# A transformer kernel on one core: the next phase's first transposes move from in front of the last six products to behind them

## The chip, the cores and the metric

The kernel runs on one NeuronCore of a Trainium2 chip. The metric is the device time of one execution in microseconds (us). The engines that matter are TensorE (PE in the profile; its weight loads are shown apart, as PEld), VectorE (DVE), ScalarE (ACT), GpSimd (POOL) and the queue of SyncE (SP), which issues most of the weight transfers.

## The reference

256 tokens of width 1024 pass through two blocks of two layers each. Cut to what matters:

```python
# first block, per layer
h = h + mixer(rms_norm(h, mix_norm_g[layer]))           # layer 0: gated chunk mixer, layer 1: dilated attention
h = h + square(relu(rms_norm(h, mlp_norm_g[layer]) @ w_up[layer])) @ w_down[layer]
...
# second block, per layer: three sub-layers, each modulated and gated by a condition
h = modulate(rms_norm(x, norm_g[i, s]), shift[:, s], scale[:, s])
x = x + gate[:, s] * sub_layer(h)                       # swiglu, then pool or conv mixer, then swiglu
```

All of it is float32. Every sub-layer begins with a norm over the 1024 values of a token, and ends with a product whose output is added to the residual stream.

## The kernel before, in words

The kernel is written engine by engine; each engine runs its own list of instructions in order, and semaphores tie them together. The 256 tokens are two tiles of 128 (t = 0 and t = 1). Weights come from HBM as slabs of 1 MB into a ring of five slots; a slot's next load is issued by the SP queue when PE has raised `slab_used`. ScalarE makes a rounded copy of a slab (`w_hi`, L498) and VectorE the remainder (`w_lo`, L831), and every product is three matmuls of 128x512 (hi by hi, hi by lo, lo by hi).

The work is a row of phases: `gate_in`, `gate_out`, `mlp0`, `qkv`, `attn`, `attn_out`, `mlp1`, `ffn0`, `pool`, `ffn1`, `ffn2`, `conv_in`, `conv_out`, `ffn3`. At the end of a phase PE finishes the accumulators `acc`: tile 0, first half of the columns, then its second half, then tile 1 in the same two halves. A half of one slab is six matmuls (two rows of weights, three matmuls each). That is `down_halves` (L1329), called from `down_last` (L1348) and at the end of `ffn` (L1652).

What follows a finished half:

- VectorE adds it to the residual stream `res` (L943; in the second block it first multiplies by the gate, L940). Each half raises `acc_ready`, the last one of all `slab_used`.
- ScalarE squares tile 0 (L518), GpSimd makes the reciprocal root (L470, L464), VectorE scales the tile into `xn` (L847) and raises `xn_ready`.
- PE transposes `xn` of tile 0 in eight transposes (`turn_norm(name, 0)`, L1388, recorded as L1376), four to a bank of `tr_ps`.
- ScalarE scales the transposed pieces back into `xn` (`norm_out`, L531 in the first block, L533 in the second), and VectorE splits them into `xT_hi` (L860) and `xT_lo` (L861), two of eight pieces at a time (`norm_split`).
- The first up product of the next phase (`first_chunk`, L1396) waits for the first two pieces (`xT_ready`), then multiplies 18 times, and then come the eight transposes of tile 1.

VectorE's list at such a border is written out in `enter` (L863). In its usual form it is:

```python
scale_tokens(NORM[name], 0)
products(1, 0)
norm_split(name, 0, (0, 2))
products(1, 1)
norm_split(name, 0, (4, 6))
scale_tokens(NORM[name], 1)
norm_split(name, 1)
```

Where `between` was given to `down_halves`, PE runs `turn_norm(next, 0)` between the two halves of tile 1: six matmuls, eight transposes, six matmuls, then the first up product. That is so at six borders: into `mlp0`, `qkv`, `mlp1`, `ffn2`, `conv_in` and `ffn3`. At two borders, into `ffn0` (where `early` is False) and into `ffn1`, the transposes already follow the last product.

Of the kernel before, what the change touches and what calls it, by code (L numbers as in the profile page):

```python
# [159 lines left out]
def build(nc, x, mix_norm_g, mlp_norm_g, final_norm_g, a_w_in, a_ln_g, a_ln_b, a_w_s, a_b_s, a_w_out,  # L160
# [7 lines left out]
    with ctx:  # L168
# [16 lines left out]
        xT_hi = sb("xT_hi", [P, KT, TOKENS], F32R)  # L185
        o_tok = nc.alloc_sbuf_tensor_at("o_tok", [P, TT, HEADS * HD], F32, offset=xT_at)
        xT_lo = sb("xT_lo", [P, KT, TOKENS], F32R)
# [3 lines left out]
        hT_hi = sb("hT_hi", [P, 4, TOKENS], F32R)  # L191
        hT_lo = sb("hT_lo", [P, 4, TOKENS], F32R)
# [62 lines left out]
        hi_ready, lo_ready, slab_used = sem("hi_ready"), sem("lo_ready"), sem("slab_used")  # L255
# [33 lines left out]
        XT = {n: i for i, n in enumerate(n for n in XN if n not in ("pool", "final2"))}  # L289
# [992 lines left out]
        def _(pe):  # L1282
# [43 lines left out]
                                      stop=stop and q == DOWNK - 1 and x_part is lo)  # L1326
                return last

            def down_halves(g, t, hi, lo, k0, between=None):  # L1329

                for c in range(2):
                    if c and between is not None:
                        between()
                    last = down_tile(g, t, hi, lo, k0, False, (c,), True)
                    if (t, c) != (TT - 1, 1):
                        last.then_inc(acc_ready, 1)
                return last
# [7 lines left out]
                    last = down_tile(g, t, hi, lo, k0, start)  # L1345
                last.then_inc(slab_used, 1)

            def down_last(g, hi, lo, k0, start, ready=None, between=None):  # L1348


                for t in range(TT):
                    if ready is not None:
                        pe.wait_ge(tr_read, ready[0] + (t + 1) * ready[1])
                    if t == 0:
                        pe.wait_ge(lo_ready, g + 1)
                    last = down_tile(g, t, hi, lo, k0, start)
                    if t == 1:
                        last.then_inc(slab_used, 1)
                    else:
                        pe.wait_ge(lo_ready, g + 2)  # L1360
                    last = down_halves(g + 1, t, hi, lo, k0 + 2, between if t else None)
                last.then_inc(slab_used, 1)

            def bank(tr):

# [22 lines left out]
            def turn_norm(name, t):  # L1388

                for b in range(KT // FILL):  # L1390
                    pe.wait_ge(xn_ready, 4 * XN[name] + 2 * t + b + 1)
                    if (t, b) == (0, 0):
                        pe.wait_ge(tr_read, at[name].tr)
                    turn(xn, t, b * FILL, FILL, at[name].tr + (KT // FILL) * t + b)
# [24 lines left out]
            g = at["gate_in"].slab  # L1419
            first_chunk("gate_in", turned=False)  # L1420
            for c in range(1, 4):
                up_chunk(g + 2 * c, free=(gelu_done, 2 * (c - 1) + 1))
                if c == 1:
                    p = at["positions"]
# [7 lines left out]
                    for n in range(NG):  # L1432
                        c0 = n * VLEN
                        while c0 < (n + 1) * VLEN:
                            c1 = min((n + 1) * VLEN, (c0 // 512 + 1) * 512)
                            last = mm(acc[0:HEADS, c0 // D, c0 % D:c0 % D + c1 - c0], rel[:, n * HEADS:(n + 1) * HEADS],
                                      mask_sb[:, n, c0 - n * VLEN:c1 - n * VLEN], start=True, stop=True)
# [4 lines left out]
            for t in range(TT):  # L1442
                pe.wait_ge(vn_ready, t + 1)
                for q in range(GROUPS):
                    last = mm(acc[:, t, q * P:(q + 1) * P], ws_T[:, q, :], g_v[:, t, q * P:(q + 1) * P],
                              start=True, stop=True)
                last.then_inc(mix_ready, 1)
            p = at["gate_out"]
            for n in range(NORM_FILLS):
                t, b = divmod(n, KT // FILL)  # L1450
                pe.wait_ge(gated, t + 1)
                turn(xn, t, b * FILL, FILL, p.tr + n)
            for k in range(2):
                down_slab(p.slab + k, xT_hi, xT_lo, 2 * k, k == 0, (p.tr, 2))
            down_last(p.slab + 2, xT_hi, xT_lo, 4, False, (p.tr, 2), lambda: turn_norm("mlp0", 0))

            def modulation(name, sub, half):

# [6 lines left out]
                        last = nc.tensor.transpose(dst[:, f * P:(f + 1) * P], ada_acc[:, n * P:(n + 1) * P], ident)  # L1465
                    last.then_inc(tr_ready, 1)

            def mlp(name, after, early=True):
                p = at[name]
                m0 = 0 if name == "mlp0" else MLP_CHUNKS  # L1470
                g = p.slab

                def turn_mid(c, t):
                    pe.wait_ge(mlp_mid, 2 * (m0 + c) + t + 1)
                    turn(mid, t, 0, 4, mid_fill(p, name, c) + t)

                def between(s, t):
                    if (s, t) == (0, 0):
                        for t in range(TT):
                            turn_mid(0, t)  # L1480
                    elif s == 1:
                        for sub in MODS.get(name, ()):
                            modulation(name, sub, t)

                first_chunk(name)
                for c in range(1, MLP_CHUNKS - 1):
                    gb = g + 4 * c - 2
                    up_chunk(gb, (relu_done, 2 * (m0 + c - 1) + 1), between if c == 1 else None)
                    for s in range(2):
                        down_slab(gb + 2 + s, hT_hi, hT_lo, 2 * s, c == 1 and s == 0,  # L1490
                                  (mid_fill(p, name, c - 1), 1))
                    for t in range(TT):
                        turn_mid(c, t)

                c = MLP_CHUNKS - 1
                gb = g + 4 * c - 2
                up_chunk(gb, (relu_done, 2 * (m0 + c - 1) + 1))
                down_slab(gb + 2, hT_hi, hT_lo, 0, False, (mid_fill(p, name, c - 1), 1))
                pe.wait_ge(lo_ready, gb + 4)
                down_tile(gb + 3, 0, hT_hi, hT_lo, 2, False)  # L1500
                turn_mid(c, 0)
                down_tile(gb + 3, 1, hT_hi, hT_lo, 2, False).then_inc(slab_used, 1)
                turn_mid(c, 1)
                down_last(gb + 4, hT_hi, hT_lo, 0, False, (mid_fill(p, name, c), 1),
                          (lambda: turn_norm(after, 0)) if early else None)
                if not early:
                    turn_norm(after, 0)

            mlp("mlp0", "qkv")

            p = at["qkv"]
# [10 lines left out]
            for i in range(2):  # L1522
                for b in range(3):
                    c = 3 * i + b
# [61 lines left out]
            pe.wait_ge(o_ready, 2 * HEADS)  # L1586
            for t in range(TT):
                turn(o_tok, t, 0, 4, p.tr + t, order=flip[:, 0, :])
            down_last(p.slab, hT_hi, hT_lo, 0, True, (p.tr, 1), lambda: turn_norm("mlp1", 0))

            mlp("mlp1", "ffn0", False)

            def gate(sub):

# [8 lines left out]
            def ffn(name, after):  # L1603
                p = at[name]
                f0 = FFN_AT[name] * FFN_CHUNKS
                g = p.slab
                mods = MODS.get(name, ())

                def turn_mid(c, t):
                    pe.wait_ge(ffn_mid, 2 * (f0 + c) + t + 1)  # L1610
                    turn(mid, t, 0, 2, mid_fill(p, name, c) + t)

                def between(s, t):
                    if (s, t) == (0, 0):
                        for m in GATES[name]:
                            gate(m)
                        for t in range(TT):
                            turn_mid(0, t)
                    elif t != s:
                        for m in mods[:1]:  # L1620
                            modulation(name, m, s)

                first_chunk(name)
                for c in range(1, FFN_CHUNKS - 1):
                    gb = g + 3 * c - 1
                    up_chunk(gb, (ffn_mid, 2 * (f0 + c - 1) + 1), between if c == 1 else None)
                    if c == 1:

                        pe.wait_ge(gate_ready, GATES[name][-1] + 1)
                        for m in mods[1:]:  # L1630
                            modulation(name, m, 0)
                    down_slab(gb + 2, hT_hi, hT_lo, 0, c == 1, (mid_fill(p, name, c - 1), 1))
                    if c == 1:
                        for m in mods[1:]:
                            modulation(name, m, 1)
                    for t in range(TT):
                        turn_mid(c, t)

                c = FFN_CHUNKS - 1
                gb = g + 3 * c - 1  # L1640
                up_chunk(gb, (ffn_mid, 2 * (f0 + c - 1) + 1))
                ready = mid_fill(p, name, c - 1)
                turn_mid(c, 0)
                pe.wait_ge(lo_ready, gb + 3)
                down_tile(gb + 2, 0, hT_hi, hT_lo, 0, False)
                turn_mid(c, 1)
                pe.wait_ge(lo_ready, gb + 4)
                pe.wait_ge(tr_read, ready + 3)
                down_halves(gb + 3, 0, hT_hi, hT_lo, 2)
                down_tile(gb + 2, 1, hT_hi, hT_lo, 0, False).then_inc(slab_used, 1)  # L1650
                pe.wait_ge(tr_read, ready + 4)
                down_halves(gb + 3, 1, hT_hi, hT_lo, 2,  # L1652
                            (lambda: turn_norm(after, 0)) if after in XT else None).then_inc(slab_used, 1)

            ffn("ffn0", "pool")
            p = at["pool"]
# [55 lines left out]
                pe.wait_ge(conv_lo, k + 1)  # L1712
                down_slab(g + k, xT_hi, xT_lo, 2 * k, k == 0)
            pe.wait_ge(conv_lo, 4)
            down_last(g + 2, xT_hi, xT_lo, 4, False, between=lambda: turn_norm("ffn3", 0))
            ffn("ffn3", "final2")


# [23 lines left out]
```

## Time and profile before

| | |
|---|---|
| median of 3 runs | 1597.26 us (1595.93 to 1598.85) |
| the profiled execution: its time | 1596.6 us |
| the profiled execution: its span | 1594.8 us |
| PE busy | 1523.5 us, 96% of the span |
| VectorE, ScalarE, GpSimd busy | 66%, 45%, 2% |
| mean granted TensorE clock | 0.984 of full |

The span is the time from the first to the last instruction of the profiled execution; 1.8 us lie around it. A busy PE is not a PE at its peak: a matmul is counted from its start to its end, and the next begins before that end.

### The profile page before, as it was taken

How to read it: one execution, taken by the hardware profiler on the slowest of the kernel's cores; microseconds unless marked ns; L12 is line 12 of the kernel's file. 1: busy time of each engine (PE TensorE's matmuls, PEld its weight loads, DVE VectorE, ACT ScalarE, POOL GpSimd, SP SyncE). 2: the span in 40 equal slices, each digit the busy share in tenths (PEclk: the TensorE clock that was granted, in tenths of full speed). 3: DMA queues.
4: the chain of work that ended last, by engine and by line, in shares of the span. 5: the costliest groups of instructions: out<-in, count | busy, mean ns of one | idle time of the engine just before them, and what ended most of it. 6: DMA issues, size and time to landing. Idle time of an engine off the chain costs nothing.

```text
span 1594.8 us, 17438 instructions
## 1 busy us (share of the span) xinstructions
PE 1523.5 (96%) x7069; PEld 1249.8 (78%) x7069; DVE 1047.8 (66%) x1220; ACT 713.4 (45%) x879; POOL 32.9 (2%) x63
## 2 busy tenths in 40 slices
PE   5999999999899999899999799999999999999998
PEld 4778888888787888678888678887788878778886
DVE  5658766645448677577888668788644465774444
ACT  6345444533444454444343434445344454454442
POOL 1000000000000000000000000000000000000000
PEclk9999999999899999999999899999999999999999
DMA  7449777557326877748988168987455555355552
GB/s 258 160 147 327 272 265 281 173 171 251 125 69 243 290 290 271 249 138 303 322 297 282 52 228 309 324 296 264 140 185 185 187 174 193 134 183 185 185 186 91
DMA packets 202203, 346.19 MB, mean 217 GB/s; under 512 B 9563, under 2 KB 105059, under 8 KB 202124
## 3 DMA queue, kind: packets, MB, share of 16 engines
q1 hardware_dynamic: 161708, 267.22, 48.7%
q10 hardware_dynamic: 40416, 77.86, 13.5%
q8 instruction: 56, 0.92, 0.2%
q14 instruction: 23, 0.19, 0.0%
HBM read 343.96 MB, written 1.09 MB: 216 GB/s over the span
## 4 chain that ended last, share of the span: by engine, by line
PE 80%; DVE 9%; DMA 4%; ACT 3%; issue 1%; POOL 1%; SPq 0%; DVEq 0%; POOLq 0%; ACTq 0%
PE up_ps L1284 48%; PE acc L1284 27%; PE tr_ps L1376 3%; DVE w_lo L831 3%; DMA raw<-in_ffn_w_in 2%; ACT w_hi L498 2%; PE tr_ps L1284 1%; DVE ada_acc L904 1%; DMA raw<-in_w_down 1%; DVE res L943 1%; DVE xn L940 1%; DMA raw<-in_w_up 1%; PE tr_ps L1558 1%; ACT xn L518 1%; DVE xT_lo L861 1%
## 5 line engine op out<-in xcount | busy, mean ns | idle before, releaser
L831 DVE TENSOR_TENSOR w_lo<-raw,w_hi 128x2048 fp32r<-128x2048 f32 x245 | 559.3, 2289 | 289.9 <-ACT w_hi L498 289.7
L498 ACT ACTIVATE w_hi<-raw 128x2048 fp32r<-128x2048 f32 x245 | 469.1, 1918 | 287.8 <-DMA raw<-in_ffn_w_in 132.3
L1284 PE MATMUL up_ps<-w_hi,xT_hi 128*128 128x512 f32 x1264 | 504.1, 399 | 13.4 <-DVE xT_lo L861 7.4
L1284 PE MATMUL up_ps<-w_hi,xT_lo 128*128 128x512 f32 x1264 | 495.5, 392 | 0.0
L1284 PE MATMUL up_ps<-w_lo,xT_hi 128*128 128x512 f32 x1264 | 494.9, 392 | 0.0
L1284 PEld LDWEIGHTS up_ps<-w_hi,xT_hi 128*128 128x128 f32 x1264 | 239.2, 189 | 67.6 <-issue 9.5
L1284 PEld LDWEIGHTS up_ps<-w_hi,xT_lo 128*128 128x128 f32 x1264 | 238.8, 189 | 51.4
L1284 PEld LDWEIGHTS up_ps<-w_lo,xT_hi 128*128 128x128 f32 x1264 | 239.5, 189 | 47.0
L1284 PE MATMUL acc<-w_hi,hT_hi 128*128 128x512 f32 x624 | 199.9, 394 | 5.7 <-DVE hT_lo L841 5.7
L1284 PE MATMUL acc<-w_hi,hT_lo 128*128 128x512 f32 x624 | 197.9, 391 | 0.0
L1284 PE MATMUL acc<-w_lo,hT_hi 128*128 128x512 f32 x624 | 197.7, 391 | 0.0
L904 DVE SCALAR_TENSOR_TENSOR ada_acc<-ada_raw,cond,ada_acc 128x512 f32<-128x512 f32 x252 | 189.1, 751 | 12.8 <-DMA ada_raw<-in_ada_w 5.1
L1284 PEld LDWEIGHTS acc<-w_hi,hT_hi 128*128 128x128 f32 x624 | 117.1, 189 | 30.2 <-DVE hT_lo L841 5.6
L508 ACT ACTIVATE hT_hi<-tr_ps 128x256 fp32r<-128x256 f32 (+1 forms) x122 | 48.3, 441 | 199.1 <-PE tr_ps L1376 195.5
L1284 PEld LDWEIGHTS acc<-w_hi,hT_lo 128*128 128x128 f32 x624 | 117.7, 189 | 24.8
L1284 PEld LDWEIGHTS acc<-w_lo,hT_hi 128*128 128x128 f32 x624 | 117.8, 189 | 24.5
L732 ACT ACTIVATE pre<-up_ps 128x256 f32<-128x256 f32 x88 | 33.4, 382 | 142.8 <-PE up_ps L1284 142.6
L841 DVE TENSOR_TENSOR hT_lo<-tr_ps,hT_hi 128x256 fp32r<-128x256 f32 (+1 forms) x122 | 55.7, 492 | 46.0 <-ACT hT_hi L508 45.5
L1138 DVE TENSOR_TENSOR mid<-pre,up_ps 128x256 f32<-128x256 f32 x88 | 35.0, 415 | 49.6 <-ACT pre L732 49.6
L518 ACT ACTIVATE xn<-res 128x512 f32<-128x512 f32 x48 | 30.6, 638 | 56.7 <-DVE res L943 48.6
L1376 PEld LDWEIGHTS tr_ps<-flip,mid 128*128 128x128 f32 x304 | 36.8, 140 | 14.1 <-issue 4.2
L1376 PE MATMUL tr_ps<-flip,mid 128*128 128x128 f32 x304 | 44.5, 273 | 2.7 <-DVE mid L1138 1.4
(123 smaller groups left out, 810.4 us busy)
## 6 DMA issues: line engine op xcount, KB each, us to landing
raw<-in_ffn_w_in SPq DMA_DIRECT2D x176, 512.0 KB, 4.8
ada_raw<-in_ada_w ACTq DMA_DIRECT2D x72, 1024.0 KB, 7.1
raw<-in_ffn_w_out SPq DMA_DIRECT2D x88, 512.0 KB, 4.4
raw<-in_w_up SPq DMA_DIRECT2D x64, 512.0 KB, 5.4
raw<-in_w_down SPq DMA_DIRECT2D x64, 512.0 KB, 4.3
raw<-in_b_w_qkv SPq DMA_DIRECT2D x36, 512.0 KB, 4.4
raw<-in_conv_w_in SPq DMA_DIRECT2D x24, 512.0 KB, 4.5
raw<-in_a_w_in SPq DMA_DIRECT2D x16, 512.0 KB, 7.5
```

The source lines that it names most:

```text
L498: nc.scalar.activation(w_hi[:, slot, :], raw[:, slot, :], ACT.Copy).then_inc(hi_ready, 1)
L508: nc.scalar.activation(dst, src, ACT.Copy).then_inc(tr_hi, 1)
L518: nc.scalar.activation(xn[:, t, cols], res[:, t, cols], ACT.Square, scale=D ** -0.5, accum_out=sumsq[:, t, c:c + 1]).then_inc(sumsq_ready[ ...
L732: nc.scalar.activation(pre[:, t, 0:HALF], up_ps[:, t, 0:HALF], ACT.Silu).then_inc(silu_done, 1)
L831: nc.vector.tensor_tensor(w_lo[:, slot, :], raw[:, slot, :], w_hi[:, slot, :].bitcast(F32), ALU.subtract).then_inc(lo_ready, 1)
L841: nc.vector.tensor_tensor(lo, src, hi.bitcast(F32), ALU.subtract).then_inc(tr_read, 1)
L861: nc.vector.tensor_tensor(lo, src, hi.bitcast(F32), ALU.subtract).then_inc(xT_ready, 1)
L904: a = nc.vector.scalar_tensor_tensor(out=dst, in0=src, scalar=cond[:, k:k + 1], in1=dst, op0=ALU.mult, op1=ALU.add)
L940: own(nc.vector.scalar_tensor_tensor(out=xn[:, t, cols], in0=src, scalar=gate, in1=gate_B[:, sub % 3, cols], op0=ALU.mult, op1=ALU.mult))
L1138: nc.vector.tensor_tensor(mid[:, t, 0:HALF], pre[:, t, 0:HALF], up_ps[:, t, HALF:UPN], ALU.mult).then_inc(ffn_mid, 1)
L1284: return nc.tensor.matmul(dst, a, b, start=start, stop=stop, skip_group_check=True)
L1376: last = nc.tensor.transpose(dst[:, q * P:(q + 1) * P], tile, ident)
```

## The change

`down_halves` loses its argument `between`, so that all twelve matmuls of tile 1's two halves stand one behind the other. `turn_norm(next, 0)` is called after them: in `down_last` through the new argument `after`, at the end of `ffn` directly. The argument `early` of `mlp` goes, because both orders are now the same. The six borders named above change; the ones into `ffn0`, `pool` and `ffn1` stay as they were. No instruction is added or taken away, and no other engine's list changes.

```diff
-            def down_halves(g, t, hi, lo, k0, between=None):
+            def down_halves(g, t, hi, lo, k0):
                 for c in range(2):
-                    if c and between is not None:
-                        between()
                     last = down_tile(g, t, hi, lo, k0, False, (c,), True)
                     if (t, c) != (TT - 1, 1):
                         last.then_inc(acc_ready, 1)
...
-            def down_last(g, hi, lo, k0, start, ready=None, between=None):
+            def down_last(g, hi, lo, k0, start, ready=None, after=None):
...
-                    last = down_halves(g + 1, t, hi, lo, k0 + 2, between if t else None)
+                    last = down_halves(g + 1, t, hi, lo, k0 + 2)
                 last.then_inc(slab_used, 1)
+                if after is not None:
+                    turn_norm(after, 0)
...
-            down_last(p.slab + 2, xT_hi, xT_lo, 4, False, (p.tr, 2), lambda: turn_norm("mlp0", 0))
+            down_last(p.slab + 2, xT_hi, xT_lo, 4, False, (p.tr, 2), "mlp0")
...
-                          (lambda: turn_norm(after, 0)) if early else None)
-                if not early:
-                    turn_norm(after, 0)
+                          after)
...
-                down_halves(gb + 3, 1, hT_hi, hT_lo, 2,
-                            (lambda: turn_norm(after, 0)) if after in XT else None).then_inc(slab_used, 1)
+                down_halves(gb + 3, 1, hT_hi, hT_lo, 2).then_inc(slab_used, 1)
+                if after in XT:
+                    turn_norm(after, 0)
```

The calls for `mlp1` and `ffn3` change in the same way as the one for `mlp0`.

## Rows read from the trace of the kernel before

**Rows 1.** Page, the chain that ended last: shares of the span by engine

```profile
PE 80%; DVE 9%; DMA 4%; ACT 3%; issue 1%; POOL 1%; SPq 0%; DVEq 0%; POOLq 0%; ACTq 0%
```

**Rows 2.** Chain in order of time, border into `mlp0`: start us, us, what

```profile
106.64 0.87 PE tr_ps L1376 x8
107.52 1.39 PE acc L1284 x6
```

**Rows 3.** Timeline, border into `mlp0`: start us, us, engine, line, what, count, idle before

```profile
106.03 0.39 PE L1284 MATMUL acc<-w_lo,xT_hi 128*128 128x512 f32 x1
...
106.25 0.39 PE L1284 MATMUL acc<-w_hi,xT_lo 128*128 128x512 f32 x1
...
106.48 1.03 PE L1376 MATMUL tr_ps<-flip,xn 128*128 128x128 f32 x8
...
107.27 0.47 PE L1284 MATMUL acc<-w_hi,xT_hi 128*128 128x512 f32 x1
...
107.78 0.29 DVE L860 CAST xT_hi<-xn 128x256 fp32r<-128x256 f32 x1 [0.41 <-ACT xn L531]
...
108.64 0.19 PEld L1284 LDWEIGHTS up_ps<-w_hi,xT_hi 128*128 128x128 f32 x1 [0.17 <-issue]
108.74 0.41 PE L1284 MATMUL up_ps<-w_hi,xT_hi 128*128 128x512 f32 x1
```

**Rows 4.** Timeline, border into `ffn3`, PE and VectorE

```profile
1394.85 0.39 PE L1284 MATMUL acc<-w_hi,xT_lo 128*128 128x512 f32 x1
...
1395.12 1.09 PE L1376 MATMUL tr_ps<-flip,xn 128*128 128x128 f32 x8
...
1396.09 0.69 DVE L943 TENSOR_TENSOR res<-res,xn 128x512 f32<-128x512 f32 x1
...
1397.62 0.47 PE L1284 MATMUL up_ps<-w_hi,xT_hi 128*128 128x512 f32 x1
```

**Rows 5.** Timeline, border into `conv_in`, PE and VectorE

```profile
1295.59 0.39 PE L1284 MATMUL acc<-w_hi,hT_lo 128*128 128x512 f32 x1
...
1296.96 1.09 PE L1376 MATMUL tr_ps<-flip,xn 128*128 128x128 f32 x8 [0.98 <-DVE xn L847]
...
1297.93 0.69 DVE L943 TENSOR_TENSOR res<-res,xn 128x512 f32<-128x512 f32 x1
```

**Rows 6.** Timeline, border into `ffn2`, PE

```profile
1095.90 0.39 PE L1284 MATMUL acc<-w_hi,hT_lo 128*128 128x512 f32 x1
...
1097.30 1.09 PE L1376 MATMUL tr_ps<-flip,xn 128*128 128x128 f32 x8 [1.01 <-DVE xn L847]
```

**Rows 7.** Timeline, border into `ffn0`, where the transposes already stand last, PE

```profile
671.41 1.09 PE L1376 MATMUL tr_ps<-flip,xn 128*128 128x128 f32 x8 [1.18 <-DVE xn L847]
...
673.90 0.47 PE L1284 MATMUL up_ps<-w_hi,xT_hi 128*128 128x512 f32 x1 [1.40 <-DVE xT_lo L861]
```

**Rows 8.** Chain in order of time, start of `mlp1`

```profile
484.16 0.33 SPq L331
...
484.53 7.24 DMA raw<-in_w_down
```

**Rows 9.** Timeline, start of `mlp1`, ScalarE's queue and PE's two waits

```profile
480.05 0.38 ACTq L567 DMA_DIRECT2D ada_raw<-in_ada_w  x1
...
496.79 1.16 PE L1465 MATMUL tr_ps<-flip,ada_acc 128*128 128x128 f32 x8 [0.89 <-DVE hT_lo L841]
...
503.21 1.60 PE L1465 MATMUL tr_ps<-flip,ada_acc 128*128 128x128 f32 x8 [2.49 <-DVE mod_sum L915]
```

**Rows 10.** Timeline, second chunk of `ffn3`, PE

```profile
1411.38 0.47 PE L1284 MATMUL up_ps<-w_hi,xT_hi 128*128 128x512 f32 x1 [1.18 <-DVE mid L1138]
```

**Rows 11.** Windows: stretch, us, busy of PE, PEld, DVE, ACT, POOL, granted clock, DMA share, GB/s

```profile
672.00:676.00 4.00, 2.60 (x11) 2.02 (x10) 1.38 (x4) 3.84 (x11) 0.00 (x0) 0.80 0.94 349
676.00:680.00 4.00, 2.83 (x9) 1.91 (x9) 2.51 (x6) 1.66 (x6) 1.17 (x3) 0.77 0.77 309
...
1296.00:1300.00 4.00, 3.04 (x17) 2.37 (x18) 3.48 (x9) 2.29 (x7) 0.38 (x1) 1.00 0.69 256
```

More of the change, by code:

```diff
@@ L1466, in modulation, with mlp @@
                     last.then_inc(tr_ready, 1)
-            def mlp(name, after, early=True):
+            def mlp(name, after):
                 p = at[name]
@@ L1588, in _ @@
                 turn(o_tok, t, 0, 4, p.tr + t, order=flip[:, 0, :])
-            down_last(p.slab, hT_hi, hT_lo, 0, True, (p.tr, 1), lambda: turn_norm("mlp1", 0))
-            mlp("mlp1", "ffn0", False)
+            down_last(p.slab, hT_hi, hT_lo, 0, True, (p.tr, 1), "mlp1")
+            mlp("mlp1", "ffn0")
             def gate(sub):
@@ L1714, in _ @@
             pe.wait_ge(conv_lo, 4)
-            down_last(g + 2, xT_hi, xT_lo, 4, False, between=lambda: turn_norm("ffn3", 0))
+            down_last(g + 2, xT_hi, xT_lo, 4, False, after="ffn3")
             ffn("ffn3", "final2")
```

## The prediction

> **What bounds the kernel now.** I read the page first, for the chain that ended last: 80% of the span lies on PE [rows 1]. So a microsecond in which PE has nothing to issue is a microsecond of the kernel, unless a later wait of PE takes it up. Then I asked for the chain in order of time at each of the eight borders between phases, and for the timeline of every engine there. In the first block (`mlp0`, `qkv`, `mlp1`) the chain runs through PE alone: eight transposes, six matmuls, the next phase [rows 2]. At the six matmuls' side ScalarE and VectorE turn the transposes' results into the first pieces of `xT`, and these are ready just as the six end: the weight load of the first up product waits 0.17 us, the product itself starts at the usual pitch [rows 3]. At the borders into `ffn2` and `conv_in` it is otherwise: PE waits 1.01 and 0.98 us for VectorE's `xn` before the transposes can begin [rows 5, 6]. Last I read PE's waits in the 40 us behind each border, for anything that could take up a delay.
>
> **The unit of the sum.** Matmuls of 128x512 in a stream start 0.225 us apart (106.03 to 106.25, and 106.48 for what follows) [rows 3]. Six of them are 6 x 0.225 = 1.35 us. From the first transpose to the first up product it is 108.74 - 106.48 = 2.26 us in `mlp0` [rows 3], and 1397.62 - 1395.12 = 2.50 us in `ffn3` [rows 4]. The second is the longer because there a scale and a shift are applied. I call this stretch the chain: transposes, ScalarE, VectorE. Before, six matmuls lay inside it. After, they lie in front of it, and nothing lies inside but the transposes.
>
> **What is removed, added and moved.** No instruction goes or comes. Six times, eight transposes move behind six matmuls on PE's list. No DMA is issued by them, and no list of another engine changes. The first up product of the next phase then starts at: start of the transposes now, plus how much later they start, plus the chain.
>
> - `mlp0`, `qkv`, `mlp1`. `xn` is ready when PE comes to the transposes (no wait stands at 106.48, and VectorE has gone on to `res`) [rows 3]; the pattern is the same three times. After, the transposes start 1.35 us later and the chain is as long as now: +1.35 us each, 4.05 us. The chain's bare length is not shown here, since the matmuls end with it. From below: the weight load at 108.64 is 0.10 us ahead of the product, of which 0.03 would remain, so at least 2.19 us [rows 3] and +1.28 us each. From above: `ffn0`, where nothing covers the chain already, has 673.90 - 671.41 = 2.49 us [rows 7], with the extra shift in it: +1.58 us each. I take 1.35, because the row of the same border is nearer than that of another kind of phase, and because the first matmul after a wait lasts 0.47 us where it lasts 0.41 in a stream [rows 3, 4], which gives back what the lower bound saves.
> - `ffn3`. The six would run from 1394.85 + 0.225 to 1396.43; the transposes start 1.31 us later than at 1395.12 [rows 4]. Eight transposes straight behind matmuls take 1.03 us [rows 3], behind a wait 1.09 [rows 4], so the chain is about 0.06 shorter: +1.25 us.
> - `ffn2` and `conv_in`. Here the six matmuls fill a wait that PE has anyway. In `conv_in` they end at 1295.59 + 0.225 + 1.35 = 1297.17 against a start of the transposes at 1296.96: +0.21 us [rows 5]. In `ffn2` they end at 1095.90 + 1.58 = 1097.48 against 1097.30: +0.18 us [rows 6]. Against that stands that VectorE is busy with the product of the half before until 1297.93 + 0.69 = 1298.62 [rows 5], so part of it is hidden, and the transposes start faster behind matmuls. Bounds 0 and 0.2; I take 0.1 each, 0.2 together. What PE won in front of the transposes it gives back behind them.
>
> Sum: 4.05 + 1.25 + 0.2 = 5.5 us. With all low bounds 3 x 1.28 + 1.25 = 5.1 us, with all high ones 3 x 1.58 + 1.31 + 0.39 = 6.4 us.
>
> **What comes after a border.** The transposes of tile 1 stand 18 up matmuls behind the first up product, and VectorE's list puts the last half's residual behind the first split of tile 0. All of it moves by the same amount, and I find nothing that catches up. The last half is finished earlier by the transposes' share: it ends at 108.91 now [rows 2], and would at 106.48 + 5 x 0.225 + 0.39 = 108.00. So the last slot of the ring comes free 0.9 us earlier, and its load starts earlier while PE starts later. No PE wait in this trace is shown to hang on that load (see the second rival).
>
> **Rivals.**
>
> - The waits at the start of `mlp1` take up that border's delay. PE waits 0.89 and 2.49 us there [rows 9]. If what it waits for did not move, 1.35 us would vanish and the sum be 4.1 us: 1601.4 us. Against it: the chain leads from the second wait back to a transfer that SP issues at 484.16, when a slab of the new phase is released, and which takes 7.24 us behind the 2 MB that ScalarE's queue asked for from 480.05 on [rows 8, 9]. Both issues follow the border and move with it. Chance 0.1.
> - The other side, not slower: weights decide behind the border. If the earlier release of 0.9 us counted at the waits of `mlp1` and at the 1.18 us wait in `ffn3` [rows 9, 10], PE would leave them 0.9 us earlier than now instead of 1.35 and 1.25 later, and the sum would be 1.35 + 1.35 - 0.9 - 0.9 + 0.2 = 1.1 us: 1598.4 us, no measurable difference. It decides once more than 2.3 of the 5.5 us are taken up. Against it: the same issue time as above, and in `ffn3` PE waits for `mid` of VectorE, whose list leads back to the border. Chance 0.06.
> - The bare waits cost clock. At `ffn0`, where PE waits 1.18 us, transposes for 1.09 and waits 1.40 [rows 7], the granted clock reads 0.80 and 0.77 over the next 8 us: part of it at 1.2 GHz instead of 2.4, a loss of 4 x 0.20 + 4 x 0.23 = 1.7 us of work [rows 11]. At the changed borders PE would transpose for about 1.03 and wait for about 1.2 to 1.4 us. One border would add 1.7 (1604.5 us), the four that now wait bare 6.8 (1609.6 us). Against it: `conv_in` has the mirror image now, a wait of 0.98 and then the transposes, at a full clock [rows 5, 11]. Chance 0.1. [...]
>
> **How the numbers follow.** The profiled execution took 1596.6 us (span 1594.8, 1.8 around it), 0.7 below the median of 1597.26. Against its own time the change gives 1602.1 us; against the median 1597.3 + 5.5 = 1602.8 us, which I forecast, with a chance of 0.72 and a range of its own from 1601.0 to 1605.0 (the bounds 5.1 and 6.4, and the spread of the three runs, about 1.5 us either way). The remaining 0.02 is for causes I don't see. A measurement of this kernel can tell about 0.2%, or 3.2 us, from no change; 5.5 us is 0.34%. The first rival is still slower, the second within 0.2%, the third slower. Some of the forecast's and of the first rival's cases fall under 3.2 us by the spread of runs. That makes 0.85 slower, 0.12 within, 0.03 faster. For the range, I go down past the first rival to 1599.3 and up to one or two borders with a lower clock, 1607.0.
>
> **What the profile would show.** At 106 us PE should issue twelve matmuls without a break, then eight transposes, and then have an idle stretch of about 1.2 us ended by `xT_lo` of VectorE, four times (`mlp0`, `qkv`, `mlp1`, `ffn3`). At `ffn2` and `conv_in` the wait for `xn` of about 1 us should be gone and one of some 1.3 us stand behind the transposes. The busy time of PE should hardly change. The start of the phases should move by 1.35, 2.7, 4.05, 4.15, 4.25 and 5.5 us. Wrong would prove me: waits behind a border that shrink by what the border lost, a first up product that starts less than 2.1 us behind the first transpose, or a granted clock below 1 right behind a changed border.

## The result, and the profile after

The kernel after takes 1605.78 us in the median of 10 runs (1600.53 to 1608.47), the kernel before 1598.01 us in 10 runs beside it (1594.7 to 1602.66). The ratio is 1.0040, with a 95% interval of 1.0023 to 1.0058: slower by 0.4%. Timed a second time (`e5_after_again` below) it was 1.0030 (1.0017 to 1.0042). The forecast was 1602.8 us with a range of 1599.3 to 1607.0, or 0.34% slower.

The page of the profiled execution of after, which took 1606.02 us:

```profile
span 1604.3 us, 17438 instructions
...
PE 1524.5 (95%) x7069; PEld 1251.6 (78%) x7069; DVE 1048.5 (65%) x1220; ACT 715.7 (45%) x879; POOL 32.9 (2%) x63
...
PE 81%; DVE 8%; DMA 5%; ACT 3%; issue 1%; POOL 0%; SPq 0%; DVEq 0%; POOLq 0%; ACTq 0%
```

The same number of instructions, the same busy time on PE, a longer span: the added time is time in which PE waits. The chain in order of time shows it at the border into `mlp0`, where it had run through PE alone [rows 2]:

```profile
99.80 7.71 PE acc L1284 x34
107.51 0.45 PE tr_ps L1376 x4
...
107.98 0.64 ACT xn L531 x2
...
108.64 0.30 DVE xT_hi L860
...
108.97 0.44 DVE xT_lo L861
...
109.54 2.51 PE up_ps L1284 x10
```

Now the chain leaves PE after the first bank of four transposes, goes through two ScalarE instructions and two of VectorE, and comes back. PE's timeline there, which answers to [rows 3]:

```profile
107.12 0.39 PE L1284 MATMUL acc<-w_hi,xT_lo 128*128 128x512 f32 x1
107.35 1.03 PE L1376 MATMUL tr_ps<-flip,xn 128*128 128x128 f32 x8
109.51 0.19 PEld L1284 LDWEIGHTS up_ps<-w_hi,xT_hi 128*128 128x128 f32 x1 [1.37 <-issue]
109.54 0.47 PE L1284 MATMUL up_ps<-w_hi,xT_hi 128*128 128x512 f32 x1 [1.16 <-DVE xT_lo L861]
...
109.85 0.39 PE L1284 MATMUL up_ps<-w_lo,xT_hi 128*128 128x512 f32 x1
```

And at the borders into `conv_in` and `ffn3`, which answer to [rows 5] and [rows 4]:

```profile
1303.85 0.40 PE L1284 MATMUL acc<-w_hi,hT_lo 128*128 128x512 f32 x1
1304.08 1.04 PE L1376 MATMUL tr_ps<-flip,xn 128*128 128x128 f32 x8
1306.52 0.47 PE L1284 MATMUL up_ps<-w_hi,xT_hi 128*128 128x512 f32 x1 [1.40 <-DVE xT_lo L861]
...
1404.35 0.40 PE L1284 MATMUL acc<-w_hi,xT_lo 128*128 128x512 f32 x1
1404.58 1.04 PE L1376 MATMUL tr_ps<-flip,xn 128*128 128x128 f32 x8
1407.02 0.47 PE L1284 MATMUL up_ps<-w_hi,xT_hi 128*128 128x512 f32 x1 [1.40 <-DVE xT_lo L861]
```

In `conv_in` the wait of 0.98 us in front of the transposes [rows 5] is gone, and one of 1.40 us stands behind them. Below, a wait in which PE has nothing at all to issue is called bare.

**A ruler for one border.** Single executions of either kernel spread over 8 us, so one span says little about 1.35 us. GpSimd's timeline is a better ruler: at each border it makes the root of tile 0 before the changed place and the root of tile 1 behind it, and the distance of the two is that border's length, whatever happened earlier. At `mlp0`, first before, then after:

```profile
104.53 0.56 POOL L464 TENSOR_TENSOR rstd<-msq,neg_half 128x1 f32<-128x1 f32 x1
...
111.28 0.56 POOL L464 TENSOR_TENSOR rstd<-msq,neg_half 128x1 f32<-128x1 f32 x1
```

```profile
104.03 0.56 POOL L464 TENSOR_TENSOR rstd<-msq,neg_half 128x1 f32<-128x1 f32 x1
...
112.15 0.56 POOL L464 TENSOR_TENSOR rstd<-msq,neg_half 128x1 f32<-128x1 f32 x1
```

6.75 us became 8.12: + 1.37 us. The same reading at all six borders, for after and for every experiment (us added against before):

| kernel | mlp0 | qkv | mlp1 | ffn2 | conv_in | ffn3 | sum |
|---|---|---|---|---|---|---|---|
| after | 1.37 | 1.36 | 1.36 | 0.16 | 0.16 | 1.35 | 5.76 |
| e5_after_again | 1.38 | 1.37 | 1.36 | 0.15 | 0.15 | 1.35 | 5.76 |
| e1_first_block | 1.38 | 1.36 | 1.37 | 0.01 | 0.01 | 0.01 | 4.14 |
| e2_ffn2_conv_in | 0.01 | 0.00 | 0.00 | 0.14 | 0.17 | 0.01 | 0.33 |
| e3_three_behind | 0.69 | 0.69 | 0.68 | 0.01 | 0.01 | 0.67 | 2.75 |
| e4_filled | 1.37 | 1.36 | 1.36 | 0.16 | 0.16 | 1.35 | 5.76 |
| e6_filled_again | 1.37 | 1.36 | 1.37 | 0.18 | 0.16 | 1.35 | 5.79 |
| e7_twelve_behind | 1.02 | 1.00 | 1.02 | 3.31 | 2.24 | 2.23 | 10.82 |
| e8_before_kept_busy | 0.01 | 0.01 | 0.01 | 0.01 | 0.01 | 0.01 | 0.06 |
| e9_after_kept_busy | 1.37 | 1.37 | 1.37 | 0.15 | 0.14 | 1.35 | 5.75 |

Where one of these six borders was left unchanged, it repeats to 0.01 us. That holds as long as the clock is full between the two roots: at the border into `ffn1`, which no kernel here changes, the distance of 7.46 us in before is 0.46 us shorter in e4 and in e7, and the granted clock there reads 0.50 and 0.68 in before (900 to 904 and 904 to 908 us). The span of after is 1604.3 - 1594.8 = 9.5 us longer in these two executions; 5.76 us of it stand at the six borders, and 3.7 us in stretches whose instructions are the same.

### The profile page after: what moved, and what is told of

It reads as the page before. It is cut to its first block, busy times and chain, and to the rows that moved or that the text cites. A ratio compares the mean times of both kernels' runs of the same rounds, so it can differ in the third digit from the quotient of the medians.

```text
span 1604.3 us, 17438 instructions
## 1 busy us (share of the span) xinstructions
PE 1524.5 (95%) x7069; PEld 1251.6 (78%) x7069; DVE 1048.5 (65%) x1220; ACT 715.7 (45%) x879; POOL 32.9 (2%) x63
## 3 DMA queue, kind: packets, MB, share of 16 engines
HBM read 343.96 MB, written 1.09 MB: 215 GB/s over the span
## 4 chain that ended last, share of the span: by engine, by line
PE 81%; DVE 8%; DMA 5%; ACT 3%; issue 1%; POOL 0%; SPq 0%; DVEq 0%; POOLq 0%; ACTq 0%
PE up_ps L1284 47%; PE acc L1284 29%; PE tr_ps L1376 3%; DVE w_lo L831 2%; DMA raw<-in_ffn_w_in 2%; ACT w_hi L498 1%; DVE ada_acc L904 1%; PE tr_ps L1284 1%; DMA raw<-in_w_down 1%; DMA ada_raw<-in_ada_w 1%; DMA raw<-in_w_up 1%; PE tr_ps L1556 1%; DVE xT_lo L861 1%; ACT xn L533 1%; DVE res L943 1%
```

## The experiments

The theory: each border costs the matmuls that no longer cover the chain from the first transpose to the first up product, and nothing where they fill another wait. The rivals: waits farther on take it up; weights decide; the bare waits cost clock. The times are in this table; ratios are to the kernel before, run beside. An uncertainty, here and below, is half the width of a 95% interval of a difference of means.

| kernel | median us (runs) | ratio, 95% interval |
|---|---|---|
| e1_first_block | 1600.65 (12) | 1.0018 (1.0003 to 1.0032) |
| e2_ffn2_conv_in | 1601.07 (12) | 1.0007 (0.9995 to 1.0018) |
| e3_three_behind | 1600.63 (12) | 1.0010 (0.9998 to 1.0022) |
| e4_filled | 1602.28 (12) | 1.0022 (1.0010 to 1.0034) |
| e5_after_again | 1603.73 (11) | 1.0030 (1.0017 to 1.0042) |
| e6_filled_again | 1602.28 (12) | 1.0020 (1.0008 to 1.0032) |
| e7_twelve_behind | 1610.24 (6) | 1.0070 (1.0054 to 1.0086) |
| e8_before_kept_busy | 1590.04 (6) | 0.9952 (0.9937 to 0.9967) |
| e9_after_kept_busy | 1597.12 (11) | 0.9991 (0.9981 to 1.0001) |
| e10_after_all_kept_busy | 1596.07 (12) | 0.9978 (0.9968 to 0.9988) |
| e11_before_kept_busy_again | 1588.89 (7) | 0.9935 (0.9921 to 0.9949) |
| e12_before_more_busy | 1586.32 (6) | 0.9928 (0.9913 to 0.9943) |

### e1_first_block: three borders only

```diff
 # kernel before; last_turn is True but for the call that leads to ffn3
-                    last = down_halves(g + 1, t, hi, lo, k0 + 2, between if t else None)
+                    last = down_halves(g + 1, t, hi, lo, k0 + 2, between if t and not last_turn else None)
                 last.then_inc(slab_used, 1)
+                if last_turn and between is not None:
+                    between()
```

> Only the three borders of the first block (mlp0, qkv, mlp1) have the transposes behind the last product; ffn2, conv_in and ffn3 keep the old order. If each border costs the six matmuls that no longer cover the chain (the theory), each of the three moves what follows by 1.36 us, read at GpSimd's two roots on either side of the border, 4.1 us together, and the other three by nothing. If waits behind a border take the delay up, the roots of the next phase are less than the sum behind. If clock is what the change costs, the lower clock is granted at or right behind these three borders. Time: before + 4.1 us by the first, + 2.7 if mlp1's waits take theirs up, + 9 if the clock falls at each.

The ruler: 1.38, 1.36 and 1.37 us, and 0.01 at the three others. The median time is 2.6 us above before, within an interval of 0.5 to 5.1 us that holds the 4.1. Each border pays for itself alone.

### e2_ffn2_conv_in: the two borders with a wait of their own

```diff
 # kernel before
-                down_halves(gb + 3, 1, hT_hi, hT_lo, 2,
-                            (lambda: turn_norm(after, 0)) if after in XT else None).then_inc(slab_used, 1)
+                down_halves(gb + 3, 1, hT_hi, hT_lo, 2).then_inc(slab_used, 1)
+                if after in XT:
+                    turn_norm(after, 0)
```

> Only the borders into ffn2 and conv_in have the new order. The six matmuls fill a wait of about 1 us that PE has there anyway, and the bare wait behind the transposes is 1.4 us, the longest of all. The theory: + 0.16 us at each border, + 0.3 us in all, so no difference that can be measured. If a bare wait costs by itself (clock, restart of PE), the time is 1.7 us or more above before for each border at which it happens, 3.4 for both, and the granted clock falls below 1 right behind them.

0.14 and 0.17 us, and a time that can't be told from before. The same six matmuls cost 1.36 us at one border and 0.15 at another; what differs is whether PE stood there anyway.

### e3_three_behind: half the cover

```diff
 # kernel before: between() is called in down_tile, before the last row of weights of the last half
+                    if q == DOWNK - 1 and mid_call is not None:
+                        mid_call()
```

> At all six borders the transposes stand in front of the last three matmuls, half way between the old order and the new one. The chain from the first transpose to the first up product is 2.19 us bare in the first block and 2.50 in the second, and three matmuls cover 0.68 us of it. The theory: each of mlp0, qkv, mlp1 and ffn3 loses 0.6 to 0.7 us, ffn2 and conv_in nothing (the transposes still wait for xn), 2.6 us in all. If any order other than the old one costs the full amount (a bare wait as such), it is 5 us or more; if the cost is only the position of the last half's residual, nothing, since VectorE does it later anyway.

0.69, 0.69, 0.68 and 0.67 us, half of 1.36, and 0.01 at the two borders with a wait of their own. PE's timeline at `mlp0`:

```profile
106.31 1.03 PE L1376 MATMUL tr_ps<-flip,xn 128*128 128x128 f32 x8
107.10 0.47 PE L1284 MATMUL acc<-w_hi,xT_hi 128*128 128x512 f32 x1
...
107.64 0.40 PE L1284 MATMUL acc<-w_hi,xT_lo 128*128 128x512 f32 x1
108.50 0.48 PE L1284 MATMUL up_ps<-w_hi,xT_hi 128*128 128x512 f32 x1 [0.47 <-DVE xT_lo L861]
```

From the first transpose to the first up product it is 2.19 us again, now with three matmuls inside and a wait of 0.47. Three matmuls moved cost 0.69 us and six cost 1.37, 0.23 us for each.

### e4_filled and e6_filled_again: useless work in the bare wait

```diff
 # kernel after, behind turn_norm(after, 0) at the six changed borders
+                    for _ in range(4):
+                        mm(up_ps[:, 0, :], w_hi[:, slot, 0:P], w_hi[:, slot, 0:512], start=True, stop=True)
```

> The new order at all six borders, with four matmuls of 128x512 without use set behind the transposes; they write a bank of up_ps that the first up product starts anew, so that the result is the same. They last 0.9 us and fit in the bare wait of 1.16 to 1.40 us. The theory: nothing changes against the new order, before + 5.8 us, 24 matmuls for nothing. If the bare waits cost clock, the filled ones give it back: 1 to 3 us less than the new order, and a mean granted clock as before. If the wait is not bare (PE is slow to restart, or the chain is slower beside matmuls), the time goes up by up to 0.9 us for each border, 5.4 in all.

> The new order with four matmuls without use in each of the six bare waits, once more, in the same call as the new order. Theory: the same time as the new order within the spread, before + 5.8 us, and the same shifts at the borders. If bare waits cost clock, 2 us or more below the new order.

```profile
108.70 1.03 PE L1378 MATMUL tr_ps<-flip,xn 128*128 128x128 f32 x8
109.49 1.17 PE L1284 MATMUL up_ps<-w_hi 128*128 128x512 f32 x4
110.89 0.47 PE L1284 MATMUL up_ps<-w_hi,xT_hi 128*128 128x512 f32 x1 [0.23 <-DVE xT_lo L861]
```

2.19 us once more, and the borders as long as in after to 0.03 us: 24 matmuls for nothing, so the wait was bare. The times lie somewhat below the new order's, 1.0022 and 1.0020 against 1.0040 and 1.0030. Where both were timed side by side, the means are 1601.9 (e6) and 1603.3 us (e5), 1.3 us apart, with an uncertainty of 1.6.

### e5_after_again

> The new order once more, unchanged, so that it is timed in the same call as the filled one. The borders alone give before + 5.8 us. If the new order also costs clock elsewhere, as its first profiled execution may hint (9.5 us longer than before, 5.75 of it at the borders), its mean lies 2 us or more above that, with a lower mean granted clock than before's 0.983.

Mean 1603.3 us against 1598.6 of before, + 4.7 us, with mean granted clocks of 0.9825 and 0.9828. The two timings of after put it at 1.0040 and 1.0030; the borders alone, 5.76 of 1598 us, are 1.0036. Most of the excess of the first profiled execution does not return.

### e7_twelve_behind: the other direction

```diff
 # kernel before, down_halves
-                    if c and between is not None:
+                    if not c and between is not None:
                         between()
```

> The transposes stand in front of both halves of tile 1, twelve matmuls before the end, one step beyond the old order. Now xn decides: PE comes to the transposes 1.35 us earlier and waits. First block: xn's first half is ready about 0.5 us after PE comes, so + 0.4 to 0.6 us at each of the three borders, since PE has no idle time there to win back. In ffn3 PE would wait 1.35 us and have all twelve matmuls behind: + 1.1 us; in ffn2 and conv_in the wait grows to 2.4 us and twelve matmuls (2.7 us) lie behind a chain of 2.5: + 1.1 us each. In all + 4.5 to 5 us. If a longer cover is always better (the cost is only what lies bare behind the transposes), no loss, or a gain of 0.3 us at ffn2, conv_in and ffn3.

The slowest of all, and the borders lost twice what I expected: 1.0 us instead of 0.4 to 0.6 at each border of the first block, 2.2 instead of 1.1 in `conv_in` and `ffn3`. PE and then VectorE at `mlp0`:

```profile
105.75 1.10 PE L1376 MATMUL tr_ps<-flip,xn 128*128 128x128 f32 x8 [0.39 <-DVE xn L847]
...
109.23 0.39 PE L1284 MATMUL acc<-w_hi,xT_lo 128*128 128x512 f32 x1
109.77 0.47 PE L1284 MATMUL up_ps<-w_hi,xT_hi 128*128 128x512 f32 x1 [0.15 <-DVE xT_lo L861]
```

```profile
108.27 0.69 DVE L943 TENSOR_TENSOR res<-res,acc 128x512 f32<-128x512 f32 x1 [2.19 <-PE acc L1284]
108.88 0.28 DVE L860 CAST xT_hi<-xn 128x256 fp32r<-128x256 f32 x1
```

I had costed PE's wait for `xn` and forgotten VectorE's list. `products(1, 0)` stands in front of the first split, and it needs the half that is now multiplied behind the transposes. VectorE idles 2.19 us for it, and the split that PE waits for comes behind. At the borders of the first block the old place suits both lists: `xn` is just ready, and the half that VectorE takes next is just done. Of the four places tried (twelve, six, three and no matmuls behind the transposes) it is the cheapest; places between six and twelve were not tried. At `ffn2` 3.31 us were added against 2.24 in `conv_in`; there the granted clock over 1104 to 1112 us was 0.79, behind a wait of 2.42 us in front of the transposes; `conv_in` waited 2.39 us and kept 1.00.

### e8_before_kept_busy and e11: the clock by itself

The longer stretches at a lower clock in the trace of before lie in or behind waits of PE (3.33 us at 80 us, 3.88 at 407, 3.74 at 657, 4.46 at 881 and 3.32 at 900). To see what they cost, the old order was given useless matmuls in those waits.

```diff
 # kernel before
+            def keep(n, dst=up_ps[:, 0, :]):
+                for _ in range(n):
+                    mm(dst, xT_hi[:, 0, 0:P], xT_hi[:, 0:2, :].rearrange("p k n -> p (k n)"), start=True, stop=True)
...
+            keep(16, acc[:, 0, 0:512])               # in front of attention
+            keep(3 + 7 * t, acc[:, 0, 0:512])        # in front of each half of mlp1's modulation
+            keep(14)                                 # in front of mlp1's last products
+            keep(5)                                  # in front of ffn0's transposes
+            pe.wait_ge(tr_read, p.tr)
+            keep(16, bank(p.tr))                     # in front of pool's products
+            keep(14, tr_ps[:, at["ffn1"].tr % 2, :]) # in front of ffn1's transposes
```

> The old order, with 82 matmuls of 128x512 without use where PE waits anyway: in front of attention (16), in the first half of mlp1 (3 and 10), in front of its last products (14), at the border into ffn0 (5), in front of pool's products (16) and at the border into ffn1 (14 plus none behind). They write banks that the next product starts anew. Theory of the clock: every stretch at half clock in the profile of before follows one of these waits, 47.8 us at half clock in all, of which some 10 to 12 us of matmul work is lost; filled waits keep the clock, and the time falls by 3 to 8 us below before, the granted clock rises above 0.983. If the clock has other causes or PE is not the bound there, no change; where the fillers do not fit into the wait, up to 0.23 us more for each that sticks out.

> The old order kept busy once more, in the same call as the new order kept busy, so that the two are compared on one chip. About 1590.5 us and a mean granted clock of 0.99 as at its first run, some 8 us below before.

These are 78 matmuls (the 82 in the first expectation is a slip of addition, and its "every stretch" leaves out the one at 80 us, behind a wait that was not filled). Faster than before by 0.48% and 0.65%, or 8 and 10 us, with 78 matmuls more: at the upper end of the 3 to 8 us expected, and above it. Windows of before, then of this kernel (stretch, length, busy of PE, PEld, DVE, ACT, POOL, granted clock, DMA share, GB/s):

```profile
76.00:92.00 16.00, 11.78 (x53) 9.84 (x52) 11.26 (x23) 4.19 (x5) 0.00 (x0) 0.79 0.11 41
404.00:426.00 22.00, 17.82 (x77) 14.14 (x78) 12.10 (x22) 12.40 (x21) 0.00 (x0) 0.69 0.28 98
652.00:694.00 42.00, 33.12 (x137) 25.39 (x136) 25.91 (x38) 24.88 (x43) 3.69 (x8) 0.92 0.52 175
872.00:916.00 44.00, 33.34 (x190) 29.42 (x189) 30.68 (x56) 19.23 (x41) 3.96 (x8) 0.84 0.22 73
```

```profile
404.00:426.00 22.00, 19.42 (x98) 15.67 (x97) 11.52 (x23) 11.23 (x22) 0.00 (x0) 0.77 0.23 82
652.00:694.00 42.00, 35.38 (x153) 26.34 (x152) 28.11 (x40) 23.98 (x45) 3.70 (x8) 1.00 0.46 159
872.00:916.00 44.00, 39.00 (x219) 31.70 (x218) 31.78 (x55) 22.40 (x45) 2.84 (x6) 1.00 0.28 90
```

In this execution 0.92 and 0.84 became 1.00. The stretch at 76 us was left alone and keeps its 0.79 (the same row in e8). It is not so in every execution: e11, the same kernel, has 0.96 from 872 to 916 us, and e12 below has 0.96 in both:

```profile
652.00:694.00 42.00, 37.24 (x160) 28.44 (x160) 27.65 (x40) 23.10 (x42) 3.72 (x8) 0.96 0.42 145
872.00:916.00 44.00, 39.20 (x213) 32.25 (x212) 31.51 (x55) 22.51 (x41) 2.85 (x6) 0.96 0.23 73
```

Behind the border into `ffn0` one wait of 2.8 us stays unfilled in all of them. The clock fell behind it in e12 (wait until 672.32 us, 0.72 and 0.85 over 672 to 680) and in e9, but not in e8 and e11. What is shown is the gain of all the filled waits together, not the price of any one.

### e9 and e10: the new order, kept busy

The same 78 matmuls in the kernel after (e9), and four more behind the transposes of each changed border (e10).

> The new order at the six borders, with the same 78 matmuls without use in PE's old waits as in the old order kept busy. Those waits no longer throw the clock back, so that the price of the order is seen with less spread. The theory: 5.8 us above the old order kept busy, in the time as well as in the sum of the shifts at the borders. If part of what the new order costs is clock that its bare waits lose, it is more, and the granted clock falls behind a border.

> The same, and four more matmuls without use in each of the six bare waits behind the transposes. The theory: the same time as without these four, to 0.5 us. If the bare waits cost clock, 1.5 us or more less.

The six borders of e9 sum to 5.75 us. The means are 1597.2 us for e9, 1595.7 for e10, and 1590.2 over the 13 runs of e8 and e11: 7.1 us for the new order, with an uncertainty of 1.7, and 5.5 us, uncertainty 1.8, with the bare waits filled. Against e11 alone, which was timed beside e9, the new order costs 7.7 us, uncertainty 2.5. So the cost agrees with what the borders show, and the bare waits cost perhaps 1.5 us more (e9 less e10, uncertainty 1.3; mean granted clock 0.9905 against 0.9912). It is the same sign and size as between e5 and e6, and both together give 1.5 us with an uncertainty of 1.0.

### e12_before_more_busy: the fastest

e8 with 12 more in front of `gate_out`'s transposes and 4 and 6 at the start of attention.

> The old order kept busy, with 22 more matmuls without use: 12 in the wait of 3.3 us in front of gate_out's transposes, 4 and 6 in the two waits at the start of attention. Behind these waits the last two longer stretches at half clock begin (6.8 us at 80 us, 10.2 us at 411 us). If the clock follows the waits, both shrink or vanish: 1 to 4 us less than the old order kept busy, some 1587 us, granted clock 0.993 or more. If PE is not the bound in attention, only the first counts, 0.5 to 2 us less.

```profile
76.00:92.00 16.00, 13.78 (x71) 11.10 (x71) 10.77 (x22) 4.08 (x5) 0.00 (x0) 1.00 0.18 60
404.00:426.00 22.00, 20.50 (x122) 16.68 (x121) 11.09 (x26) 11.41 (x23) 0.00 (x0) 0.92 0.24 77
```

0.79 became 1.00 and 0.69 became 0.92. 1586.32 us is 0.72% below before and 1.1% below after (0.9928 over 1.0035, the middle of after's two ratios), with 100 matmuls for nothing. It is the version that beats both.

## Why the prediction was right, and where it was off

- **The unit, six matmuls or 1.35 us: right.** 1.36 to 1.38 us at the three borders of the first block, half of it in `e3_three_behind`.
- **The chain's bare length: the lower bound was the truth.** I took 2.26 us; it is 2.19 (107.35 to 109.54), the figure worked out from the weight load that stood 0.10 us ahead of the product [rows 3]. The 0.03 us that the prediction left between weight load and product had no row there; after shows it (109.51 and 109.54). The border still lost 1.37 and not 1.28 us: the transposes start 1.37 us later behind the first root (3.32 against 1.95), the chain is 0.07 shorter, and the second up product starts 0.31 us after the first, 0.24 in before. The last two cancel, as argued.
- **`ffn3`: 1.25 forecast, 1.35 measured.** The chain did get shorter by 0.06 (2.44 from 1404.58 to 1407.02, against 2.50). What was short is the start of the transposes, forecast 1.31 us later; behind the first root it moved by 1.40:

```profile
1393.98 0.56 POOL L464 TENSOR_TENSOR rstd<-msq,neg_half 128x1 f32<-128x1 f32 x1
...
1400.98 0.56 POOL L464 TENSOR_TENSOR rstd<-msq,neg_half 128x1 f32<-128x1 f32 x1
```

```profile
1402.04 0.56 POOL L464 TENSOR_TENSOR rstd<-msq,neg_half 128x1 f32<-128x1 f32 x1
...
1410.39 0.56 POOL L464 TENSOR_TENSOR rstd<-msq,neg_half 128x1 f32<-128x1 f32 x1
```

  In before it is 1395.12 - 1393.98 = 1.14 us [rows 4], in after 1404.58 - 1402.04 = 2.54. A slower restart has no part in it: the second up product follows the first after 0.30 us in before and 0.31 in after. The prediction counted from the last matmul in front of the transposes, 1394.85, which is 0.87 us behind the root; in e2, e8 and e11, with the old order at this border too, it is 0.95. Of the terms this was the one furthest off.
- **`ffn2` and `conv_in`: 0.1 forecast, 0.16 measured each,** inside the bounds of 0 and 0.2. The wait in front of the transposes went, one of 1.40 us came behind. The transposes start 0.21 us later, as worked out, and the chain is 0.05 to 0.06 shorter (2.44 against 2.49), which is the faster start of the transposes that the prediction named. VectorE's list, its other reason for taking half of the bound, hides nothing.
- **The sum: 5.5 us forecast, 5.76 measured** at the borders; 7.8 us between the medians of the first timing, 5.6 between those of the second (1603.73 and 1598.16).
- **First rival, `mlp1`'s waits take the delay up: not so.** PE's two waits there are 1.55 and 2.49 us in after, against 0.89 and 2.49 [rows 9]; they did not shrink. From the second root at `mlp1` to the first at `ffn0` it is 190.11 us in after, 190.12 in e1, 188.64 in e4, 188.65 in e5 and 189.02 in e6, against 189.38 in before and 188.54 in e2: no 1.35 us are gone. In after the first wait is 0.66 us longer, as much as the transfer it hangs on (7.91 us instead of 7.24 [rows 8]). Yet something gives a little back: e4 and e6, the new order with its bare waits filled, are 3.4 us slower than before in the mean (uncertainty about 1.0), less than the 5.8 at their borders. Where these 2 us go no single place of the traces shows.
- **Second rival, weights decide: wrong.** No changed border and neither of `mlp1`'s waits got shorter, and the time is not the 1598.4 us that it gives.
- **Third rival, clock: not at the size forecast, perhaps at a small one.** No changed border is followed by a lower clock, as a forecast of 1.7 us for each would need: in the profiled executions of after, e1, e2, e5 and e9 the granted clock reads 1.00 over the 20 us behind each. But filling the bare waits gave 1.3 and 1.5 us in two independent comparisons, the first not clear by itself, the second just (uncertainties 1.6 and 1.3). Where in the kernel that is lost no trace shows. The price of 1.7 us, read at `ffn0`, was not a fixed one either. PE waits 1.18 and 1.40 us there in e3 and e4 as well, and the clock stays full:

```profile
672.73 1.09 PE L1376 MATMUL tr_ps<-flip,xn 128*128 128x128 f32 x8 [1.18 <-DVE xn L847]
...
675.22 0.47 PE L1284 MATMUL up_ps<-w_hi,xT_hi 128*128 128x512 f32 x1 [1.40 <-DVE xT_lo L861]
```

```profile
674.00:694.00 20.00, 14.65 (x65) 11.14 (x66) 14.47 (x24) 13.86 (x29) 1.98 (x4) 1.00 0.53 197
```

  That PE's waits together do cost clock, e8 and e12 show: 8 to 12 us of before.

What stays open is the size and the place of these two small terms of opposite sign. The forecast of 1602.8 us holds because its main term, the borders, is right; both timings together make the new order 5.6 us slower in the mean (uncertainty 1.4), against 5.8 at the borders. If both open terms are real, they nearly cancel there, which I had not forecast and which would be luck.

## What to carry to other kernels

A hand-over (transposes, ScalarE, VectorE, back to PE) costs PE its bare length less the independent matmuls that stand behind its first instruction; count them at the pitch of the stream, 0.225 us here, border by border, and expect nothing where PE waits for the hand-over's input anyway. Look for the earliest place at which the input is ready and at which no other engine's list is made to wait for a product that was pushed behind. And look at the granted clock around PE's waits before you look at their length: useless matmuls in waits that were left as they are gave more here than any order of the useful ones.

## What the runs showed of the hardware that I had not expected

- Useless matmuls in PE's waits made the kernel faster by 0.72% (e12). The granted clock of the profiled execution rose from 0.984 to 0.995. In before, the four windows shown above, 124 us together, hold 16 x 0.21 + 22 x 0.31 + 42 x 0.08 + 44 x 0.16 = 20.6 of the 1594.8 x 0.016 = 25.5 us of clock that were lost.
- Two waits of 1.18 and 1.40 us around transposes that lasted 1.09 us were followed at once by a lower clock in some executions (before [rows 7, 11], e5, e6), 5 us or more later in others (after, e1, e2), and not over the next 18 us in e3 and e4. One such wait beside transposes, at the six changed borders, was followed by none in any profiled execution of the new order.
- A GpSimd root has the same distance to its neighbour across two executions to 0.01 us at an unchanged border with a full clock, while the whole span of the same kernel varies by 8 us. The variation sits in a few places: transfers (7.24 against 7.91 us for the same slab) and stretches at the lower clock.
